# Splitting the value products of an attention stage into two column halves

## The reference

```python
def memory_attn(q, k, v):                 # 4 heads, 256 memory tokens, both layers
    s = jnp.einsum('bshd,bmhd->bhsm', q, k) * (D ** -0.5)
    p = jax.nn.softmax(s, axis=-1)
    o = jnp.einsum('bhsm,bmhd->bshd', p, v)
...
# layer 0: windowed_gqa, 12 query heads on 4 key/value heads, a band of up to 3 blocks of 128 keys
    p = jax.nn.softmax(jnp.concatenate([s, sink_col], axis=-1), axis=-1)[..., :-1]
    o = jnp.einsum('bkgniu,bnukd->bnikgd', p, vband)
# layer 1: neighbourhood_attn, 12 heads, 256 keys for each block of 128 queries
    o = jnp.einsum('bhrcij,brijhd->brchd', p, vband)
```

## Time and profile before

| | |
|---|---|
| median of three runs | 1996.39 us |
| time of the profiled execution | 1996.64 us |
| span of its trace | 1994.9 us |
| work outside the span | 1.7 us |
| mean granted TensorE clock | 0.998 |
| TensorE busy (matmuls) | 1970.6 us, 99% |
| VectorE busy | 1092.7 us, 55% |
| ScalarE busy | 853.5 us, 43% |
| GpSimd busy | 201.4 us, 10% |
| DMA, mean | 87 GB/s |

### The profile page before, as it was taken

The page is one execution under the profiler, slowest core; times in us unless marked ns, Lnnn a source line. Parts: engine busy times, 40 slices in busy tenths (PEclk is TensorE's granted clock), DMA queues, the critical chain, the costliest instruction groups (busy, mean ns, idle before and its releaser), DMA issues.

```text
span 1994.9 us, 31378 instructions
## 1 busy us (share of the span) xinstructions
PE 1970.6 (99%) x11631; PEld 1727.1 (87%) x11631; DVE 1092.7 (55%) x1878; ACT 853.5 (43%) x1274; POOL 201.4 (10%) x195
## 2 busy tenths in 40 slices
PE   8999999999999999999999999999999999999998
PEld 7989989999888988889988888888889888888887
DVE  6235999555653566577654433444656654433443
ACT  6224665543223554466643222234666543212333
POOL 2004111200100110001001100110014001100100
PEclk9999999999999999999999999999999999999999
DMA  4322111233333324331033332332332133323332
GB/s 140 110 83 78 53 54 54 78 92 95 90 102 107 95 84 115 107 96 42 12 95 95 99 102 84 95 110 79 103 87 65 43 95 95 108 82 95 95 101 79
DMA packets 320578, 174.21 MB, mean 87 GB/s; under 512 B 5216, under 2 KB 317920, under 8 KB 320496
## 3 DMA queue, kind: packets, MB, share of 16 engines
q1 hardware_dynamic: 320496, 173.11, 29.7%
HBM read 170.99 MB, written 2.10 MB: 87 GB/s over the span
## 4 chain that ended last, share of the span: by engine, by line
PE 95%; DVE 3%; issue 1%; ACT 1%; DMA 0%; SPq 0%; POOL 0%; POOLq 0%; DVEq 0%; ACTq 0%
PE ps L2194 54%; PE ps L2200 27%; PE ps L2812 3%; PE ps L2772 2%; PE ps L2797 2%; PE ps L2347 1%; PE ps L2408 1%; PE ps L2750 1%; PE ps L2751 1%; PE ps L2687 1%; PE ps L2441 0%; DVE w_lo L1385 0%; PE ps L2822 0%; DMA x_rows<-x 0%; PE ps L2299 0%
## 5 line engine op out<-in xcount | busy, mean ns | idle before, releaser
L2194 PE MATMUL ps<-z_hi,w_hi 128*128 128x512 f32 (+2 forms) x2032 | 623.6, 345 | 0.0
L1385 DVE TENSOR_TENSOR w_lo<-raw,w_hi 128x1024 fp32r<-128x1024 f32 (+2 forms) x298 | 385.9, 1295 | 430.3 <-ACT w_hi L829 429.0
L2194 PE MATMUL ps<-z_lo,w_hi 128*128 128x512 f32 (+2 forms) x2032 | 614.8, 341 | 0.0
L829 ACT ACTIVATE w_hi<-raw 128x1024 fp32r<-128x1024 f32 (+2 forms) x298 | 328.3, 1102 | 443.1 <-PE ps L2200 408.0
L2200 PE MATMUL ps<-z_hi,w_lo 128*128 128x512 f32 (+2 forms) x2032 | 433.0, 341 | 0.0
L2194 PEld LDWEIGHTS ps<-z_hi,w_hi 128*128 128x128 f32 x2032 | 352.0, 189 | 50.9 <-issue 3.1
L2194 PEld LDWEIGHTS ps<-z_lo,w_hi 128*128 128x128 f32 x2032 | 350.8, 189 | 44.7
L2200 PEld LDWEIGHTS ps<-z_hi,w_lo 128*128 128x128 f32 x2032 | 333.3, 189 | 45.2
L2194 PE MATMUL ps<-g_hi,w_hi 128*128 128x512 f32 (+1 forms) x539 | 209.4, 390 | 0.0
L2194 PE MATMUL ps<-g_lo,w_hi 128*128 128x512 f32 (+1 forms) x539 | 208.8, 389 | 0.0
L760 POOL TENSOR_TENSOR g_lo<-gv,g_hi 128x512 f32 x65 | 84.4, 1299 | 1062.5 <-ACT g_hi L1240 1062.5
(11 more groups left out here) (352 smaller groups left out, 2413.3 us busy)
## 6 DMA issues: line engine op xcount, KB each, us to landing
raw<-w_gate_up SPq DMA_DIRECT2D x88, 512.0 KB, 3.9
raw<-w_down SPq DMA_DIRECT2D x48, 704.0 KB, 4.8
raw<-w_in SPq DMA_DIRECT2D x44, 512.0 KB, 3.9
raw<-w_up SPq DMA_DIRECT2D x44, 512.0 KB, 3.8
raw<-w_out SPq DMA_DIRECT2D x24, 512.0 KB, 4.0
raw<-w_in_b SPq DMA_DIRECT2D x14, 512.0 KB, 3.8
raw<-w_in_a SPq DMA_DIRECT2D x12, 512.0 KB, 3.8
raw<-w_branch SPq DMA_DIRECT2D x8, 512.0 KB, 3.9
```

Of the source, the lines that this page charges most:

```text
L829: act.activation(w_hi[s][:, 0:width], raw[s][:, 0:width], ACT.Copy).then_inc(hi_done, 1)
L1385: dve.tensor_tensor(w_lo[s][:, 0:width], raw[s][:, 0:width], w_hi[s][:, 0:width].bitcast(F32), ALU.subtract).then_inc(lo_done, 1)
L2194: pe.matmul(out, w_hi[s][:, w0 + k * P:w0 + (k + 1) * P], rhs[:, lo:lo + width], start=a, stop=False)
```

## The change

Each value product becomes two: the first takes columns 0 to 63 of the turned probabilities as weights and writes partitions 0 to 63 of the bank, the second takes columns 64 to 127 and writes partitions 64 to 127. Both stream the same 65 columns of values. The order of all work stays, and so do the waits and the increment, which is now on the second half of the last product.

```diff
@@ -2182,6 +2182,12 @@
+            def column_halves(out, weights, moving, start, stop):
+
+                for t in range(2):
+                    x = pe.matmul(out[t * VD:(t + 1) * VD], weights[:, t * VD:(t + 1) * VD], moving, start=start, stop=stop)
+                return x
+
@@ -2809,8 +2815,8 @@
-                        x = pe.matmul(y_bank(r)[:, b * VS:(b + 1) * VS], pts[b % 2][:, j * P:(j + 1) * P], v,
-                                      start=j == 0, stop=j == width // P - 1)
+                        x = column_halves(y_bank(r)[:, b * VS:(b + 1) * VS], pts[b % 2][:, j * P:(j + 1) * P], v,
+                                          j == 0, j == width // P - 1)
                     x.then_inc(s["y"], 1)
```

## The result

The changed kernel takes 2009.72 us, median of six runs (2009.15 to 2011.39), against 1995.83 for the kernel before in its six (1995.15 to 1996.77): 13.9 us more, a ratio of 1.007 with a 95% interval of 1.0057 to 1.0083. The profiled execution took 2009.15 us with a span of 2007.4, 12.5 over the span of before. The forecast was 2010.6.

What follows compares the result with a forecast made beforehand. The prediction took TensorE to bound the kernel. From 1996.64 us it added 15.3 for switching net of faster halves, took off 1.3 of hidden waits, and forecast 2010.6 us, 0.7% slower, range 2006 to 2019.

Steps and rivals of the forecast that it cites:

- The bound: Attention, both layers: TensorE has no hole, so a loss on it is paid in full; value products some 60 us.
- Halves in a stream: Value products: a product in halves takes 0.115 us against 0.22, saving 29 us by the stream alone.
- Beginning: Switch from scores to half products: 0.15 us, giving 0.39 for runs of eight records and 0.50 for twelve.
- Ending: Switch from half products to the transposes behind: 0.14 us extra a run, bounds nothing to 0.20.
- lower bound of nothing: Ending's lower bound: no extra, as line 2430's transposes start 0.11 behind 16-column line 2428 with no hole.
- rival A: Value runs: TensorE does not empty at the switches, so 23 us saved, 1973.6 us; chance 0.06.
- Hidden waits: Value runs already waiting for their block's copy: TensorE empties there at no cost, 1.3 us taken off.
- half form: Rival A's variant at value runs: TensorE empties at one edge alone, 1992.7 us; chance 0.04.
- B: Value products: the two halves do not overlap, 2041.6 us, or 2032 in a middle form; chance 0.08 in both.
- break-even: Value runs: the change wins only if beginning and ending together cost less than 0.18 us; rows say 0.29.
- The sum: All 128 value runs: +0.14 us per run of four, +0.03 per run of six, together 15.3 us more before hidden waits.

Runs made afterwards that it cites:

- the pairs: Change regrouped against the kernel before: two value runs in halves back to back, four buffers, maxima wait behind transposes; 1992.45 us against 1996.59, ratio 0.9979.

## Why the prediction was right

**The bound.** TensorE without a hole in attention, so that everything on it is paid: the chain stays on TensorE at 95%, and the forecast of 14.0 us met 13.9 in the medians and 12.5 in the spans. That the first two agree within 0.1 us is luck: rounding of the rows alone was put at some 3 us for the sum, and one of the terms below erred by 1 us.

**Halves in a stream.** 0.058 for a pair, from line 2404. Runs of eight at 0.38 and of twelve at 0.50 have four records, two pairs, between them: 0.06 a pair. The 65th column shows in no row.

**Beginning.** 0.15 from line 2394; forecast 0.39 and 0.50 for the runs, measured 0.38 and 0.50. The first forecast was 0.01 too dear, 104 x 0.01 = 1 us.

**Ending.** This term had the widest bounds, nothing to 0.20, and the choice of 0.14 by the transposes of line 2588 held: 0.48 - 0.33 = 0.15 and 0.37 - 0.23 = 0.14. It is 128 x 0.14 = 18 us and thus larger than the whole loss; with the 0.20 of line 2194 the forecast would have been 8 us too high. What decided was to take the row with the same kind of work behind the gap, not the gap behind the same kind of product. It was one row of four transposes. The change has such groups too, in the last steps of the layers (line 2822 before, 2828 after): they take 0.585 us against 0.443 before, the same 0.14.

The lower bound of nothing was misread, and with it the one row that spoke for rival A. In rows 9 the products of line 2425 have 16 columns of weights and end at 198.78, and the 16-column transpose of line 2428 starts at 198.71, 0.07 before that end. So TensorE empties between these two, and the full-width transposes of line 2430, which start 0.16 before the end of line 2428, come after the emptying and say nothing about it. Line 2425 too starts 0.07 before the end of the full-width work ahead. The trace of before has this sequence eight times, and all agree but for one transpose that waits for something else.

**Hidden waits.** 1.3 us were taken off. The runs between transposes at 0.38 [after, chain at 980.79] show that their 0.95 went as supposed. The first run of layer 1 still waits for its copy, 0.42 us where it waited 0.59, so it gave 0.17 of the 0.24.

**The rivals.** A, no emptying, is refuted by the timelines after at both edges, and so is its half form; B by leaving one half out. The break-even that A named, 0.18 us of saving for 0.29 of switching, is what the pairs use: one switching for two runs, with four buffers, turns +13.9 into -4.1.

**The sum again.** By the rows, 104 x (0.14 - 0.01) + 24 x (0.14 - 0.11) - 1.3 = 13 us. Added up over all 128 runs in both traces, the value products take 5.1 us less and the work right behind them 18.4 more, 13.4 together. The spans differ by 12.5 and the medians by 13.9; the six times of the kernel before lie within 1.6 us of each other, so no more can be asked of the sum.

## What to carry to other kernels

Column halves nearly double the rate of these small fp32 products (0.12 us instead of 0.22), but each passage between full and half width costs about 0.15 us on either side. So count the passages, not the products: 0.29 us a group against 0.10 us a product saved puts the break-even at about three products. Split only where a group holds more, or regroup first. Regrouping costs by itself: 3 us here for loads that are no longer hidden. With the faster halves another 3 us went to copies into buffers whose readers came late, and came back in the form with twice the buffers. Where a group grew to a whole head, the chain left TensorE in part for the engines around it, and a gain that was right by count did not appear at all.

## What the runs showed of the hardware

Half of the price of a switching falls on the work behind it, under the name of an untouched line: the transposes grew from 0.33 to 0.48 us. The other half, 0.15 us ahead of the products, is hidden in the products' own row, since their saving offsets it: 0.38 us against 0.39.

Not every product of less than 128 columns empties TensorE. In the trace of before those with 64 and with 16 columns of weights start 0.07 us before the modelled end of the full-width work ahead, while one with 86 columns (line 2289, at 450.56) starts 0.16 before that end at 450.72, as in a stream.

Matmuls on different halves are not held to the order of the program: with all of one half first, eight records took 0.39 us, as when alternating, and twelve took 0.67 against 0.50, where strict order would have given 0.61 and 0.84. The Trainium skill, "TensorE: Matmul & The Clock Gate", section "The mechanism", says that matmuls start and end strictly in order; these runs show starts out of that order between halves, and the measurement decides. The same section's rule that a weight load overlaps matmuls in flight only in another row group is not borne out either: the halves share their rows, and in a run of eight four loads and products on each half took 0.38 us from end to end, 0.15 of it for emptying, though each load's record lasts 138 ns and each product's 222.
